# A two-block layer stack on one core: a quarter of the gate weights moved into head 0 of the delta rule, and the attention bias read along diagonals of a repeated table

## The reference, cut to what matters

```python
# first block
mod = silu(c) @ w_ada + b_ada                  # 3 x 2048: shift, scale, gate
u = rms_norm(h, pre_w) * (1 + scale) + shift
z, xbc, dt, qkv, b, a = split(u @ w_in)
ssd = ssd_mixer(silu(conv(xbc)), dt)           # state-space heads
gdn = gdn_mixer(silu(conv(qkv)), b, a)         # 8 heads of the delta rule
y = concat(norm(ssd * silu(z)), norm(gdn) * silu(z))
h = h + gate * rms_norm(y @ w_out, post_w)     # the gate is needed only here
# second block, attention of both layers
dist = q_pos[:, None] - k_pos[None, :]
bias = take(rel_bias, bucket(dist))            # depends on q - k alone
s = where(dist >= 0, q @ k.T * scale + bias, -1e30)
p = softmax(s); p = p[0] - lam * p[1]
```

## Time and profile before

| | us |
|---|---|
| timed runs | 3102.63, 3123.97, 3126.11 |
| median | 3123.97 |
| the profiled execution's own time | 3097.79 |
| its span | 3096.0 |
| head 0 with its lead-in | 140 to 214 |
| start of the state-space stage | 632 |
| projection | 805 to 910 |
| first layer begins | 917 |

### The profile page before, as it was taken

How to read it: one execution, slowest core, us unless ns; L and a number is a source line. 1 busy time by engine, 2 the same in 40 slices (tenths; PEclk the granted TensorE clock), 3 DMA queues, 4 the chain that set the end, 5 groups by cost and what they waited for, 6 DMA issues and landing times.

```text
span 3096.0 us, 68313 instructions
## 1 busy us (share of the span) xinstructions
PE 3011.3 (97%) x28654; PEld 2833.5 (92%) x28654; DVE 1865.4 (60%) x2520; ACT 1334.5 (43%) x1731; POOL 183.0 (6%) x282
## 2 busy tenths in 40 slices
PE   6899999999999999999999999999999999999999
PEld 2677877878889999999999999999999999999999
DVE  3566776768886666555555554566665555555544
ACT  3344554444444444444333333444444443333432
POOL 0000000000110000211000000200002110000000
PEclk8999999999999999999999999999999999999999
DMA  9621121222674544555555555554445555555554
GB/s 365 266 83 70 70 80 74 70 96 90 249 301 177 177 176 159 194 190 190 193 198 193 190 191 195 197 204 175 172 158 188 190 191 196 197 190 191 193 197 152
DMA packets 81472, 543.99 MB, mean 176 GB/s; under 512 B 8325, under 2 KB 12437, under 8 KB 17440
## 3 DMA queue, kind: packets, MB, share of 16 engines
q1 hardware_dynamic: 77808, 519.08, 46.4%
q10 hardware_dynamic: 2768, 19.66, 1.6%
q0 software_dynamic: 736, 2.90, 0.3%
HBM read 537.38 MB, written 4.22 MB: 175 GB/s over the span
## 4 chain that ended last, share of the span: by engine, by line
PE 88%; DVE 5%; issue 4%; ACT 2%; DMA 1%; POOLq 0%; DVEq 0%; SPq 0%; ACTq 0%; POOL 0%
PE bank L436 27%; PE bank L437 26%; PE bank L438 26%; PE bank L787 1%; DMA raw<-stream 1%; DVE w_lo L420 1%; PE bank L659 1%; PE bank L695 1%; PE bank L711 1%; DVE s_acc L1550 0%; DMA xr<-x_t 0%; PE bank L887 0%; PE bank L1066 0%; PE bank L712 0%; PE bank L713 0%
## 5 line engine op out<-in xcount | busy, mean ns | idle before, releaser
L415 ACT CAST w_hi<-raw 128x2048 fp32r<-128x2048 f32 x449 | 858.4, 1912 | 1243.8 <-PE bank L438 1243.1
L420 DVE TENSOR_TENSOR w_lo<-raw,w_hi 128x2048 fp32r<-128x2048 f32 x449 | 1031.5, 2297 | 551.1 <-ACT w_hi L415 550.7
L436 PE MATMUL bank<-a_lo,w_hi 128*128 128x256 f32 (+1 forms) x3600 | 1071.3, 298 | 11.3 <-DVE w_lo L420 8.5
L437 PE MATMUL bank<-a_hi,w_lo 128*128 128x256 f32 (+1 forms) x3600 | 1044.8, 290 | 0.0
L438 PE MATMUL bank<-a_hi,w_hi 128*128 128x256 f32 (+1 forms) x3600 | 1044.4, 290 | 0.0
L436 PE MATMUL bank<-h_lo,w_hi 128*128 128x256 f32 x3584 | 1000.6, 279 | 0.6
L437 PE MATMUL bank<-h_hi,w_lo 128*128 128x256 f32 x3584 | 990.3, 276 | 0.0
L438 PE MATMUL bank<-h_hi,w_hi 128*128 128x256 f32 x3584 | 990.1, 276 | 0.0
L436 PEld LDWEIGHTS bank<-a_lo,w_hi 128*128 128x128 f32 x3600 | 678.6, 189 | 34.5 <-DVE w_lo L420 10.9
L438 PEld LDWEIGHTS bank<-a_hi,w_hi 128*128 128x128 f32 x3600 | 678.3, 188 | 17.5
L437 PEld LDWEIGHTS bank<-a_hi,w_lo 128*128 128x128 f32 x3600 | 680.4, 189 | 13.3 <-issue 0.5
(11 more groups left out here) (328 smaller groups left out, 2032.7 us busy)
## 6 DMA issues: line engine op xcount, KB each, us to landing
raw<-stream SPq DMA_DIRECT2D x485, 1024.0 KB, 4.8
gate_raw<-stream ACTq DMA_DIRECT2D x16, 1024.0 KB, 7.1
xr<-x_t SPq DMA_DIRECT2D x4, 1024.0 KB, 16.2
turned<-by_distance POOLq DMA_DIRECT2D x1, 2048.0 KB, 12.5
x_res<-x_t SPq DMA_DIRECT2D x1, 2048.0 KB, 17.8
bias_table<-bias SPq DMA_DIRECT2D x1, 2048.0 KB, 11.7
bias<-bias_table ACTq DMA_DIRECT2D x1, 2048.0 KB, 9.3
out_t<-x_res SPq DMA_DIRECT2D x4, 512.0 KB, 5.2
```

The source lines that it names most:

```text
L415: act.copy(w_hi[u.slot][:], raw[u.raw][:]).then_inc(hi_ready, 1)
L420: dve.tensor_tensor(w_lo[u.slot][:], raw[u.raw][:], w_hi[u.slot][:], ALU.subtract).then_inc(lo_ready, 1)
L436: pe.matmul(acc, wh, lo[:, k, 0:n], start=(k == first), stop=False)
L437: pe.matmul(acc, wl, hi[:, k, 0:n], start=False, stop=False)
```

## The change

Gate: the units of the gate's last 512 values (four of 16) now travel through SP's stream and the ring. The order behind `FRONT` is written out in `LATER`, with the gate units after units 38 and 39; a unit's place in the ring is shifted by up to four. PE multiplies them as it does the modulation (`gate_part`): parts 0 and 1 before unit 36, part 2 behind unit 37, part 3 in level 3 of the solve of head 0, and the columns (`gate_part_columns`) in level 4. ACT copies the bank in level 3 (into `mrow[0]`), the DVE adds the bias of the modulation in level 5. The other 12 units stay where they were: the DVE sums one before each of the first three splits of every four, with its loop unrolled, and ACT loads 12. `c32` moves to a place that is not overwritten in head 0.

Bias: `turned`, the flips, ACT's copies and the permutation matrix (128 columns of the constants) go. Instead POOL copies within DRAM: `repeated` writes, for each head and map, the row of 383 values 128 times behind one another into `scratch[1]`; `diagonals` reads that with a step of 382 from partition to partition straight into `bias`. The heads are done in two groups, 5 and 3 (10 and 6 rows of the table), because `scratch[1]` holds no more. The first copy is issued behind the first barrier, ahead of the memset of `s_pad`; the first read after the last unit of the state-space stage; the second pair after POOL's last sum of the projection. SP waits for all four (`bias_table` at 64) before it writes `bias` to `scratch[1]`, now at unit 10 of the first layer instead of unit 7, and the DVE waits at the scores of the first layer.

```diff
+GATE_KEPT = 12
+LATER = [("unit", FIRST), ("unit", FIRST + 1), ("unit", FIRST + 2), ("gate", 0), ("gate", 1), ("gate", 2), ("unit", FIRST + 3),
+         ("gate", 3), *(("unit", FIRST + k) for k in range(4, 8))]
...
+PERIOD = DIST - 1
+TABLE_HEADS = 5
...
+        def repeated(h0, h1):
+
+            n = 2 * (h1 - h0)
+            return (bass.AP(scratch[1].tensor, 0, [[P * PERIOD, n], [PERIOD, P], [1, PERIOD]]),
+                    bass.AP(scratch[0].tensor, 2 * DIST * h0, [[DIST, n], [0, P], [1, PERIOD]]))
+
+        def diagonals(h0, h1):
+
+            n = 2 * (h1 - h0)
+            return (d3(bias[:, 2 * L * h0:2 * L * h1], L),
+                    bass.AP(scratch[1].tensor, P - 1, [[PERIOD - 1, P], [P * PERIOD, n], [1, L]]))
...
-            for p in range(RAW, FIRST + RAW):
+            order = FRONT + LATER
+            for p in range(RAW, len(order)):
                 free(p - RAW)
...
-                        if n == U_LAYER + 7:
-                            sp.wait_ge(S["flip_read"], 8)
+                        if n == U_LAYER + 10:
+                            sp.wait_ge(S["bias_table"], 64)
                             sp.dma_start(scratch[1], bias[:]).then_inc(S["rel_out"], 16)
...
             leave(pool, 1)
+            pool.wait_ge(S["rel_out"], 16)
+            pool.dma_start(*repeated(0, TABLE_HEADS)).then_inc(S["bias_table"], 16)
             pool.memset(s_pad[:], 0.0).then_inc(S["pads_set"], 1)
...
-            pool.wait_ge(S["rel_out"], 16)
-            pool.dma_start(d3(turned[:], L), bass.AP(scratch[0].tensor, 0, [[1, P], [DIST, 2 * HEADS], [1, L]])
-                           ).then_inc(S["turned_ready"], 16)
+            pool.wait_ge(S["bias_table"], 16)
+            pool.wait_ge(unit_done, U_WOUT)
+            pool.dma_start(*diagonals(0, TABLE_HEADS)).then_inc(S["bias_table"], 16)
...
             mixed_sum(KT // 2 - 1, 0).then_inc(S["acc_ready"], 1)
+            pool.wait_ge(S["bias_table"], 32)
+            pool.dma_start(*repeated(TABLE_HEADS, HEADS)).then_inc(S["bias_table"], 16)
+            pool.wait_ge(S["bias_table"], 48)
+            pool.dma_start(*diagonals(TABLE_HEADS, HEADS)).then_inc(S["bias_table"], 16)
...
+            def gate_part(m):
+
+                p = GATE_AT[m]
+                pe.wait_ge(raw_ready[p % RAW], (p // RAW + 1) * 16)
+                for t in range(4):
+                    last = mm(psum[5][t * B32:(t + 1) * B32, :], c32[:, (m * 4 + t) * B32:(m * 4 + t + 1) * B32],
+                              raw[p % RAW][:, t * 512:(t + 1) * 512], start=(m == 0), stop=(m == 3), skip_group_check=True)
+                last.then_inc(S["gate_part"], 1)
...
+            pe.wait_ge(S["sm_cum"], 1)
+            gate_part(0)
+            gate_part(1)
             unit_mm(pe, Unit(U_GDN + 3), u_hi3, u_lo3, L)
...
                 ahead(0, 0, KT)
+                if i == 0:
+                    gate_part(2)
...
                     m.then_inc(S["x32_mm"], 1)
+                    if i == 0 and level == 3:
+                        gate_part(3)
...
+                    if i == 0 and level == 4:
+                        gate_part_columns()
...
-            pe.wait_ge(S["turned_ready"], 16)
-
-            def flip(k):
-                if k >= 5:
-                    pe.wait_ge(S["flip_read"], k - 4)
-                mm(psum[2 + k % 5][:], K("flip"), turned[:, k * 512:(k + 1) * 512], start=True, stop=True).then_inc(S["flip_mm"], 1)
...
-                    if i < 2 and j % 2:
-                        flip(4 * i + j - 1)
-                        flip(4 * i + j)
                 gate_columns(i)
-            pe.wait_ge(S["flip_read"], 8)
...
             norm_sums(0)
-            gate_columns(KT // 4 - 1)
...
+                    if i == 0 and level == 3:
+                        act.wait_ge(S["gate_part"], 4)
+                        act.copy(mrow[0][:], psum[5][:]).then_inc(S["mrow_ready"], 1)
...
-                    if i * 4 + j < KT - 2:
-                        act.wait_ge(S["gate_used"], i * 4 + (j + 1))
-                        gate_load(i, j + 2)
+                    n = 3 * i + j
+                    if j < 3 and n + 2 < GATE_KEPT:
+                        act.wait_ge(S["gate_used"], n + 1)
+                        gate_load(n + 2)
...
+            for i in range(KT // 4):
                 for j in range(4):
+                    if j < 3:
+                        gate_sum(3 * i + j)
                     split_dve(dve, Unit(U_WOUT + j + 2, i))
...
+                    if l == 0:
+                        dve.wait_ge(S["bias_table"], 32 if isinstance(i, int) else 64)
```

More of the change, by code:

```diff
@@ L93 @@
                  28: (2, 0), 29: (2, 1)}
-CONST = {"ident": 0, "ones": P, "flip": 2 * P, "blk": 3 * P, "sel": 4 * P}
-KEEP = 4 * P + 8
+GATE_KEPT = 12
+LATER = [("unit", FIRST), ("unit", FIRST + 1), ("unit", FIRST + 2), ("gate", 0), ("gate", 1), ("gate", 2), ("unit", FIRST + 3),
+         ("gate", 3), *(("unit", FIRST + k) for k in range(4, 8))]
+GATE_AT = [FIRST + k for k, (kind, _) in enumerate(LATER) if kind == "gate"]
+CONST = {"ident": 0, "ones": P, "blk": 2 * P, "sel": 3 * P}
+KEEP = 3 * P + 8
 LEVEL = KEEP + 6 * P
@@ L144, in constants @@
     put("ones", 0, 1.0)
-    put("flip", 0, i + j == P - 1)
     put("blk", 0, i // DK == j // DK)
@@ L204, in __init__ @@
         self.n = c + i * (4 * groups)
-        self.raw = c % RAW
-        self.turn = c // RAW + i * groups
+        place = self.n + 4 if not isinstance(self.n, int) or self.n >= FIRST + 4 else FIRST + LATER.index(("unit", max(self.n, FIRST)))
+        self.raw = c % RAW if not isinstance(self.n, int) else place % RAW
+        self.turn = (c + 4) // RAW + i * groups if not isinstance(self.n, int) else place // RAW
         self.bank = {U_GDN + 1: 2, U_GDN + 2: 4}.get(self.n, c % 2) if isinstance(self.n, int) else c % 2
@@ L513, in free @@
             def free(p):
-                kind, m = FRONT[p]
+                kind, m = order[p]
                 if kind == "ada":
                     sp.wait_ge(unit_done, m + 1)
+                elif kind == "quarter":
+                    sp.wait_ge(S["q_lo"], 2 * m + 2)
+                elif kind == "unit":
+                    sp.wait_ge(lo_ready, Unit(m).split)
                 else:
-                    sp.wait_ge(S["q_lo"], 2 * m + 2)
+                    sp.wait_ge(S["gate_part"], m + 1)
             def quarter(m, r):
@@ L531, in _, with gate_unit @@
                              x_dram[r * 512:(r + 1) * 512, :].rearrange("(k p) t -> p k t", p=P)).then_inc(ld_x[r], 16)
-            for p in range(RAW, FIRST + RAW):
+            def gate_unit(m, r):
+                row = GATE_ROW + GATE_KEPT + m
+                sp.dma_start(raw[r][:], stream[row:row + 1].rearrange("a p m -> p (a m)")).then_inc(raw_ready[r], 16)
+            order = FRONT + LATER
+            for p in range(RAW, len(order)):
                 free(p - RAW)
-                kind, n = FRONT[p] if p < FIRST else ("unit", p)
-                (quarter if kind == "quarter" else load)(n, p % RAW)
-            for begin, end in ((FIRST // RAW + 1, U_BC // RAW), ((U_LAYER + 12) // RAW, N_SEQ // RAW)):
+                kind, n = order[p]
+                {"ada": load, "quarter": quarter, "unit": load, "gate": gate_unit}[kind](n, p % RAW)
+            for begin, end in ((len(order) // RAW - 1, U_BC // RAW), ((U_LAYER + 12) // RAW, N_SEQ // RAW)):
                 with sp.Fori(begin, end) as i:
@@ L753, in _, with gate_part_columns @@
             m.then_inc(S["row_mm"], 1)
+            def gate_part(m):
[5 more added lines that the diff above has]
+                last.then_inc(S["gate_part"], 1)
+            def gate_part_columns():
+                pe.wait_ge(S["mrow_ready"], 2 * PAIRS + 1)
+                for j in range(4):
+                    m = mm(psum[5][:, 504 + 2 * j:506 + 2 * j], mrow[0][:, j * P:(j + 1) * P], K("sel", 0, 2), start=True, stop=True)
+                m.then_inc(S["ada_cols"], 1)
+            pe.wait_ge(S["sm_cum"], 1)
+            gate_part(0)
+            gate_part(1)
             unit_mm(pe, Unit(U_GDN + 3), u_hi3, u_lo3, L)
@@ L1753, in head @@
                     dve.wait_ge(S["x32_mm"], i * 6 + level)
+                    if i == 0 and level == PACKED:
+                        dve.wait_ge(S["ada_cols"], 2 * PAIRS + 1)
+                        tt(mods[:, 64 + 2 * GATE_KEPT:96:2], psum[5][:, 504:512:2], par("b_ada", 32 + GATE_KEPT, 4), ALU.add)
                     if level < PACKED:
```

67 lines of the change are left out of this document (29 added, 38 removed).

## The result

The changed kernel takes 3090.67 us (median of 22 runs, 3086.49 to 3120.80), the kernel before beside it 3104.82 (22 runs, 3092.84 to 3137.70). The ratio is 0.9946 with a 95% interval of 0.9923 to 0.9969: 0.54% faster, some 17 us (10 to 24 by the interval), while the medians differ by 14.2 us. Medians and counts here are of all runs; ratios leave out the few runs over 1.5% above the fastest of their kernel. I had forecast -4.65 us. That is unchanged by the bound of 1%, as forecast, but the size is beyond the -8.3 us of my good ends, and the profiled executions show only part of it: 3097.79 and 3090.82 us, spans 3096.0 and 3089.0, -7.0 us.

A forecast was written before the change was run, and what follows sets the result against it. PE was taken to bound the kernel nearly everywhere; +0.3 (head 0) + 0.95 (state-space start) - 6.9 + 1.0 (projection) = -4.65 us, so 3093.1 against the profiled 3097.79 and 3119 against the median, range 3089 to 3131.

The forecast's parts named there:

- good ends: Favourable bounds added up: -2 in head 0, 0.6 on POOL, no delay of transfers; together -8.3 us.
- that on the stop: Head 0, solve level 3: instructions inserted ahead may move a 1.99 us PE stop into a wait or bring another; 2 us either way.
- The scaling: Whole kernel: the -4.65 us sum gave 3093.1 against the profiled 3097.79, and 3119 against the median of 3123.97.
- bad ends: Unfavourable bounds added up: +6.6 in head 0, 2.4 on POOL, 6.3 in the projection; together +8.4 us.
- Rival 4: PE stops without a releaser, 1.99 us each, appear at two or three new places: 3123 to 3125, unchanged; chance 0.10.
- Rival 1: Projection bound by transfers instead: 5.3 us more of the gain go, sum +0.65, 3125, unchanged; chance 0.18.
- Rival 2: State-space start: POOL's DRAM-to-DRAM issue takes over 5.6 us instead of 0.95; at 10 us, 3128; chance 0.08.
- Rival 3: Second table late, SP waiting for it holds the weights; only on one engine too late, 3159; chance 0.04.
- Head 0: Gate products: parts 0 to 2 hidden, part 3 and columns cost 1.8, an earlier solve gains 1.5; +0.3 us.
- State-space start: POOL issues the table DMA ahead of the s_pad memset, PE pays its time in full: +0.95 us, bounds 0.6 and 2.4.
- Projection: Flips gone, -6.9 us if PE stays the bound; late gate loads give back +1.0, bounds 0 and +6.3.
- The rule on outermost dimensions: Repeated tables: a DMA's outermost dimension under 16 caps its engines, so 10 and 6 outermost run on ten and six.

The follow-up runs named there:

- before_pad80: Kernel before plus 20 tiny unused products (80 PE instructions) at the very start; 3093.73 us, ratio 0.9967 to the kernel before.
- before_load_late: Kernel before with the heads' raw weight load waiting for one split more, PE's instructions unmoved; 3090.41 us, ratio 0.9959.
- bias_alone: Kernel before with only the bias part (no flips, repeated tables, 16 gate units in the projection); 3103.30 us, ratio 1.0001.
- bias_pad80_memset: Kernel before with the bias part, 80 dummy PE instructions at the start and POOL's first table DMA behind the memset; 3089.12 us, ratio 0.9948.
- after_memset_first: Changed kernel with POOL's first table DMA behind the memset of the padded buffer; 3090.02 us, ratio 0.9949 to the kernel before.

## Why the prediction was right or wrong

1. *The step that failed* is that on the stop: "Uncertain is a stop of 1.99 us in the middle of the products of level 3, which the trace lays to nothing but issue [...] 2 us either way". I booked one stop, in head 0, at its own length. The trace of before had a second one, in head 1, and half clock behind it: 3.5 us that the change removes, in a stretch whose code it leaves alone. In other executions there are three or four, 11 to 14 us. So the term is not ±2 but -3.5 in the profile and some -8 to -11 at the median: three late heads on the mean of six profiles, 3.7 us each, or the 10.7 and 12.3 us of before_pad80 and before_load_late less the 2.2 to 2.4 us that head 0 loses there and not in the changed kernel. What stands behind the stop, a packet of instructions held up by a weight load, the prediction did not have.
2. *The scaling failed with it.* I took the sum against the profiled execution and moved it to the median unchanged. But that profile had one late head where the others had three or four, so what the change removes is larger at the median than in it. And the median of 3123.97 was of three runs; that of 22 is 3104.82, which alone makes 19 of the 28.6 us between my 3119 and the 3090.67. That 3090.67 still lies within 3089 to 3131 is the width of the scatter, not the sum, whose bad ends on 3126 would have made the upper end 3134.
3. Rival 4 named stops without a releaser at new places; I had no case in which old ones go. Rival 1 fell: no wait for a transfer in the projection with 12 loads; with 16 and no flips the DVE's sums wait 5.6 and 5.9 us for their loads, and PE 1.6 to 2.3 us more for splits (bias_alone, bias_pad80_memset). Rival 2 fell: POOL's issue took 1.11 us. Rival 3 fell: the second table was there in time, below.
4. Head 0 was +0.3, measured -0.7 against the profile. But that profile's head 0 was long (60.5, the others 57.7 to 58.0, its clock at 0.50 for 6 us), and against these it is +1.8 to +2.1. The pieces held: parts 0 to 2 hidden, 1.8 us for part 3 and the columns (rows of 1.06 and 0.95, with the next products 0.99 and 0.81 behind their starts), the clock at 1.00 from 150 to 170, and the solve begins 12.8 us into the head instead of 14.2 (-1.4, I had -1.5). PE's wait for the keys was 1.09 us where I had put it under 1. The stop went to an earlier level of the solve and stayed. Against before_pad80, with no stop and 55.7, the gate part costs 4.1.
5. State-space start +0.95: 1.37 by PE's wait, which after_memset_first takes back. The stage's length agrees where the clock is the same (196.3 without, 197.8 with the DMA ahead); whether the clock falls in it, 1.5 us and more, my sum didn't have.
6. Projection -6.9 + 1.0 = -5.9: measured -5.0. The delay by transfers that I charged is not there. Instead 13 units took 0.21 us more than the 5.44 that I read from the earlier trace rows (5.65, last section), +2.7, which leaves some -7.7 for the flips with what stood around them. after_memset_first, where most units took 5.44 to 5.59, has 92.1 us (-8.2), but half of its 3.2 us on after are the clock: behind PE's wait of 2.2 us near 822 it stays at 1.00 there and falls to 0.50 in after, as it does in before.
7. The rule on outermost dimensions: the tables with 10 and 6 outermost landed after 12.8 and 15.8 us (the DMA view of 630 to 700 and of 902 to 935; KB each, us to landing):

```profile
bias_table<-by_distance POOLq DMA_DIRECT2D x1, 1915.0 KB, 12.8
...
bias_table<-by_distance POOLq DMA_DIRECT2D x1, 1149.0 KB, 15.8
```

By the earlier trace rows (2048 KB in 11.7 us) they would take 10.9 and 6.6 with all engines, and by the Trainium skill's "DMA: Bandwidth & Descriptors", "Rules for kernel authors", an estimated 17.5 each on ten and six. The second is near the rule's figure, the first is between, and no run has the same tables with another outermost dimension, so whether the rule is the cause is not shown. Both were in time, so it decides nothing here.

## What to carry to other kernels

Where a profile lays a stop of TensorE to issue in a run of very small products, look in the DMA view for the instruction queue: if a packet of the program stands behind a large load, any edit ahead of it, even dummy instructions, can move the time by more than the edit's own work. Compare the lengths of equal loop passes within a run and over several profiles before attributing a gain; moving the load (one changed wait) brought the median here from 3102.7 to 3090.4 us, the whole change from 3104.8 to 3090.7. And a single profiled execution below the median may lack something that the median has: find it before scaling a sum.

## What the hardware showed that I had not expected

Instruction packets queue behind weight loads: late ones began 26.9 to 27.8 us into a head, as the load that starts at 24 ended, and those in time at 20.8 to 24.7 (from the DMA view in narrow windows). A start at 27 us is not late by itself: in heads 1 to 7 of after a packet begins at 27.1 to 27.3 without a stop, but it is the next one of the program, and the one before it began at 20.9 to 23.4.

Streams of equal products run at one of two speeds, both at full clock. A unit of 48 products takes 5.44 us (113 ns a product) or 5.65 (118), and mostly keeps that for a stretch. In the projection of after it stayed at the lower speed (clock 1.00 from 830 to 875); ACT's squares, one a unit:

```profile
842.35 0.39 ACT L1472 ACTIVATE hbuf<-bank 128x256 f32<-128x256 f32 x1
848.01 0.39 ACT L1472 ACTIVATE hbuf<-bank 128x256 f32<-128x256 f32 x1
```

In the layers of before, the counts of PE's products in 20 us are 172 in one stretch and 179 behind it, the clock 1.00 in both:

```profile
2310.00:2330.00 20.00, 20.00 (x172) 20.00 (x171) 10.94 (x11) 9.27 (x8) 5.41 (x8) 1.00 0.44 158
...
2410.00:2430.00 20.00, 20.00 (x179) 20.00 (x178) 10.93 (x12) 8.11 (x7) 2.46 (x4) 1.00 0.50 177
```

That is 4%, and after has 179 in both windows. By the casts of ACT 15 units of the layers of before stand 5.65 us apart, 3.2 us more than at 5.44, and none in after, which is enough for the layers' -2.5 us above. It is no work of the change: the six profiles of before have 1 to 30 such units. What sets the speed wasn't tried.
